# A transformer block on one core: window heads in pairs, and extra tokens' products split behind each half of the gate-up units

## The reference, cut to what matters

```python
h = rms_norm(x, attn_norm);  proj = h @ w_in + b_in
sb = stick_breaking_attention(...)            # 8 heads of 64
sw = sliding_window_attention(...)            # 8 heads of 64, 2 key/value heads, 128 rows a tile, keys of 2 tiles
mixed = concat(rms_norm(sb), rms_norm(sw))
x = x + mixed @ w_out + b_out
x = x + moe(rms_norm(x))                      # 32 experts, 4 a token, 1024 -> 2 x 1024 -> 1024
out = rms_norm(x)

# sliding window, one tile of 128 queries, one head
s = q @ k.T * scale + rel_bias;  p = softmax(concat(s, sink))[..., :-1];  o = p @ v
# expert
gate, up = min(gu[:, :FF], 7), clip(gu[:, FF:], -7, 7)
act = (up + 1) * gate * sigmoid(1.702 * gate);  y = act @ w_down + b_down
```

## Time and profile before

| | us |
|---|---|
| median of 3 runs | 2323.31 |
| runs | 2319.99 to 2324.42 |
| profiled execution, its own time | 2329.55 |
| its span, first to last instruction | 2327.8 |
| TensorE busy | 2142.0 (92%) |
| VectorE busy | 1524.8 (66%) |
| ScalarE busy | 1473.9 (63%) |
| POOL busy | 333.4 (14%) |

### The profile page before, as it was taken

One profiled execution on the slowest core, in us unless ns is written; L12 is line 12 of the kernel. 1 busy time (PEld: TensorE's weight loads), 2 busy tenths in 40 slices (PEclk: granted clock), 3 DMA queues, 4 the chain that ended last, 5 costly groups with the idle time before them and its releaser, 6 DMA issues.

```text
span 2327.8 us, 36220 instructions
## 1 busy us (share of the span) xinstructions
PE 2142.0 (92%) x10647; PEld 1600.9 (69%) x10648; DVE 1524.8 (66%) x1940; ACT 1473.9 (63%) x1976; POOL 333.4 (14%) x327
## 2 busy tenths in 40 slices
PE   5999999998878399999999999999999999999997
PEld 4777777765656277778777677777776677676684
DVE  4455455544444578898879677777776677575685
ACT  4456566643332268888778677777776677575583
POOL 1000000001222211111111111121121111110112
PEclk9999999859888599999999999999999999999996
DMA  6301000111011859999799797897896898696694
GB/s 187 61 19 28 19 10 19 73 46 54 30 56 47 277 191 374 375 377 372 244 378 312 256 369 262 301 373 266 298 371 216 280 333 284 210 367 223 226 358 174
DMA packets 250410, 507.19 MB, mean 218 GB/s; under 512 B 44454, under 2 KB 62676, under 8 KB 250228
## 3 DMA queue, kind: packets, MB, share of 16 engines
q1 hardware_dynamic: 234724, 462.98, 55.2%
q0 software_dynamic: 15632, 43.53, 7.4%
HBM read 470.25 MB, written 38.54 MB: 219 GB/s over the span
## 4 chain that ended last, share of the span: by engine, by line
PE 63%; DVE 9%; DMA 8%; issue 8%; SPq 5%; ACT 4%; POOL 1%; DVEq 0%; ACTq 0%; POOLq 0%
PE bank L963 18%; PE bank L985 11%; PE bank L754 8%; PE bank L803 4%; DMA slot_in<-slot_rows 4%; PE bank L1000 3%; DVE w_low L1740 3%; PE bank L848 3%; PE bank L831 3%; DMA xg<-h_rows,gather_idx 3%; SPq L485 3%; PE bank L1006 3%; PE bank L1021 2%; PE bank L782 2%; SPq L498 1%
## 5 line engine op out<-in xcount | busy, mean ns | idle before, releaser
L1740 DVE TENSOR_TENSOR w_low<-gu_w,w_high 128x1024 fp32r<-128x1024 f32 x528 | 617.3, 1221 | 201.0 <-ACT w_high L1312 197.4
L1312 ACT CAST w_high<-gu_w 128x1024 fp32r<-128x1024 f32 x528 | 531.4, 1049 | 107.5 <-PE bank L985 76.0
L963 PE MATMUL bank<-w_high,x_high 128*128 128x512 f32 x1056 | 415.6, 394 | 2.8 <-DVE w_low L1740 2.8
L963 PE MATMUL bank<-w_high,x_low 128*128 128x512 f32 x1056 | 413.7, 392 | 0.0
L963 PE MATMUL bank<-w_low,x_high 128*128 128x512 f32 x1056 | 413.0, 391 | 0.0
L1740 DVE TENSOR_TENSOR w_low<-dn_w,w_high 128x1024 fp32r<-128x1024 f32 x264 | 315.3, 1226 | 12.1 <-ACT w_high L1312 7.2
L1312 ACT CAST w_high<-dn_w 128x1024 fp32r<-128x1024 f32 x264 | 270.7, 1050 | 18.6 <-PE bank L963 8.6
L985 PE MATMUL bank<-w_high,act_high 128*128 128x512 f32 x528 | 218.9, 415 | 14.5 <-DVE act_low L1754 14.5
L963 PEld LDWEIGHTS bank<-w_high,x_high 128*128 128x128 f32 x1056 | 198.9, 188 | 45.6 <-DVE w_low L1740 3.5
L963 PEld LDWEIGHTS bank<-w_low,x_high 128*128 128x128 f32 x1056 | 198.9, 188 | 42.7
L963 PEld LDWEIGHTS bank<-w_high,x_low 128*128 128x128 f32 x1056 | 198.7, 188 | 42.5
(11 more groups left out here) (227 smaller groups left out, 3282.2 us busy)
## 6 DMA issues: line engine op xcount, KB each, us to landing
gu_w<-in_w_gate_up SPq DMA_DIRECT2D x528, 512.0 KB, 12.3
dn_w<-in_w_down SPq DMA_DIRECT2D x132, 1024.0 KB, 18.4
w_st<-in_w_in SPq DMA_DIRECT2D x14, 512.0 KB, 4.8
xt<-in_x SPq DMA_DIRECT2D x8, 512.0 KB, 4.2
wo_sb<-in_w_out SPq DMA_DIRECT2D x2, 2048.0 KB, 9.9
x<-in_x SPq DMA_DIRECT2D x8, 512.0 KB
residual_rows<-x SPq DMA_DIRECT2D x8, 512.0 KB, 3.6
h_rows<-h SPq DMA_DIRECT2D x8, 512.0 KB
```

Source lines behind the costliest of these rows:

```text
L963: mm = pe.matmul(bank[:, 2 * h + g, :], a[:, k, :], b, start=False, stop=last)
L1312: act.copy(w_high[:, u % RING, :], src).then_inc(high_ready, 1)
L1740: dve.tensor_tensor(w_low[:, u % RING, :], raw, w_high[:, u % RING, :], ALU.subtract).then_inc(split_ready, 1)
```

## The change

The window units become pairs of heads: four steps for a tile in place of eight. `scores` writes two products into one bank, `band` (for `window`) treats both heads, `weights` has two exponents, `turn` transposes four blocks and `values` multiplies them. The work of `out_stage` is bound to steps counted from the start of its tile: `tile_at(step, after)` gives the tile for which `after` steps have passed. The mix transposes come eight steps after the start of their tile, ahead of that step's `turn`; the projection comes in four chunks of four steps (twelve matmuls each). `x2_variance` is split from `normed`, and POOL's order is shifted by one tile.

In the expert stage `over_hidden` is called once for each half: for half 0 behind the first half of units, for half 1 behind the second. With four column tiles each matmul now has 256 columns and there are twice as many; with two tiles the columns stay 512. A new semaphore `over_half` tells that half 0 is through; `refill` waits for it ahead of the first four pairs of `gu_w` loads, and for `over_psum` ahead of the other four. The wait for `y_ready` moves ahead of the first call. `over_rows` reads the gate and up columns with another view of the banks.

```diff
+BAND = NH // 2
+MIX_TURN = 2 * BAND
+LAST = BAND * (NT - 1) + 20
...
-        tD = kb("tD", [P, 2, 2, P], F32, 150)
-        tC = kb("tC", [P, 4, SPAN], F32, 162)
+        tD = kb("tD", [P, 2, 4, P], F32, 150)
+        tC = kb("tC", [P, 2, 2 * SPAN], F32, 162)
...
-        units += [(i, h, "sw") for i in range(NT) for h in range(NH)]
+        units += [(i, j, "sw") for i in range(NT) for j in range(BAND)]
...
+        def tile_at(step, after):
+            t, rest = divmod(step - after, BAND)
+            return t if rest == 0 and 0 <= t < NT else None
...
             def refill(i, e, first):
                 sp.wait_ge(d_gather, 16 * i)
                 load_slots(i, e, first)
-                sp.wait_ge(over_psum, i)
+                sp.wait_ge(over_half, i)
                 sp.sem_inc(sp_passed, 1)
                 for s in range(KT):
+                    if s == 4:
+                        sp.wait_ge(over_psum, i)
+                        sp.sem_inc(sp_passed, 1)
                     sp.wait_ge(split_ready, UNITS * i + (2 * s + 2 - UNITS))
                     load_gu(e, s)
...
-            for t in range(NT + 1):
+            for t in range(NT + 2):
                 if t < NT:
                     for n in range(2 * t, 2 * t + 2):
                         rstd(mix_var, n + 1, mix_rstd, col(40 + n), col(24 + n))
+                if t >= 2:
+                    rstd(x2_var, t - 1, x2_rstd, col(64 + t - 2), col(56 + t - 2))
+                if t < NT:
                     pool.wait_ge(d_x2[t % 2], 16 * (t // 2 + 1))
                     pool.tensor_tensor(x2[:, t % 2], x2[:, t % 2], bout_bc[:], ALU.add).then_inc(xb_ready, 1)
-                if t >= 1:
-                    rstd(x2_var, t, x2_rstd, col(64 + t - 1), col(56 + t - 1))
-                if t >= 2:
-                    write_records(t - 2)
+                if t >= 3:
+                    write_records(t - 3)
...
+                if kind == "sw":
+                    if u == SB:
+                        pe.wait_ge(proj_done, 2 * CHUNKS)
+                    k0, n = max(i - 1, 0) * P, cols // 2
+                    rows = slice(HD * (h // 2), HD * (h // 2) + HD)
+                    for a in range(2):
+                        mm = pe.matmul(out_z[:, n * a:n * a + n], qk_sw[rows, 2 * (h % 2) + a, i * P:i * P + P],
+                                       qk_sw[rows, 4, k0:k0 + n], start=True, stop=True)
...
+            def before_turn(step):
+                t = tile_at(step, MIX_TURN)
+                if t is not None:
+                    turn(("mix", t, 0))
+                    turn(("mix", t, 1))
+                for j in range(1, 4):
+                    t = tile_at(step, 9 + j)
+                    if t is not None:
+                        project(t, range(4 * j, 4 * j + 4))
...
+                else:
+                    before_turn(u - SB)
                 turn(u)
                 if u >= 1:
                     values(u - 1)
                 if u >= SB:
-                    out_stage((u - SB) // NH, (u - SB) % NH)
+                    after_values(u - SB)
...
-            def over_hidden(i, parts):
-                m = P // parts
+            def over_hidden(i, h, parts):
+                m, w = P // parts, HALF // parts
+                bias = bias_f.rearrange("p (g h f) -> p h g f", g=2, h=2)
                 for k in range(-1, KT):
-                    for g in range(parts):
+                    for q in range(parts):
                         lhs = pick_f[:, 0:m] if k < 0 else xo[:, k, 0:m]
...
+                        rhs = bias[:, h] if k < 0 else gu_w[:, h, k]
+                        mm = pe.matmul(over_view(parts)[m * q:m * q + m, h], lhs, rhs[:, :, w * q:w * q + w],
+                                       start=(k < 0), stop=(k == KT - 1))
+                mm.then_inc((over_half, over_psum)[h], 1)
...
                 hidden(i, 0, range(2, KT))
+                pe.wait_ge(y_ready, 2 * i + 2)
+                by_class(n_tok, lambda parts: over_hidden(i, 0, parts))
                 expert_bias(i, 1)
                 hidden(i, 1, range(5))
                 turn_hidden(i, 0)
                 hidden(i, 1, range(5, KT))
-                pe.wait_ge(y_ready, 2 * i + 2)
-                by_class(n_tok, lambda parts: over_hidden(i, parts))
+                by_class(n_tok, lambda parts: over_hidden(i, 1, parts))
```

More of the change, by code:

```diff
@@ L375, in program @@
                 add_groups(("v", m), 4)
+            if tile_at(u - SB, MIX_TURN) is not None:
+                for part in range(2):
+                    add_groups(("mix", tile_at(u - SB, MIX_TURN), part), 4)
             add_groups(u, blocks(u))
-            if u >= SB and (u - SB) % NH == 5 and u - SB >= NH:
+        for step in range(STEPS, LAST):
+            if tile_at(step, MIX_TURN) is not None:
                 for part in range(2):
-                    add_groups(("mix", (u - SB) // NH - 1, part), 4)
-        for part in range(2):
-            add_groups(("mix", NT - 1, part), 4)
+                    add_groups(("mix", tile_at(step, MIX_TURN), part), 4)
         def proj_bank(n):
@@ L915, in _ @@
                 if u >= SB:
-                    out_stage((u - SB) // NH, (u - SB) % NH)
-            values(NU - 1)
-            for t in range(NT, NT + 3):
-                for h in range(NH):
-                    out_stage(t, h)
+                    after_values(u - SB)
+            for step in range(STEPS, LAST):
+                before_turn(step)
+                if step == STEPS:
+                    values(NU - 1)
+                after_values(step)
             for s in range(NT):
@@ L1504, in keep_out, with band @@
                 dve.tensor_copy(o_sb[:, i, P * p:P * p + P], bank[:, 6, 0:P]).then_inc(o_kept, 1)
-            def window(u):
-                i, h, _ = units[u]
-                n = blocks(u) * P
-                tc = tC[:, u % 4, 0:n]
+            def band(u):
+                i, j, _ = units[u]
+                n = blocks(u) * P // 2
                 dve.wait_ge(z_ready, u + 1)
@@ new lines, in out_stage @@
+            def out_stage(step):
+                if step == 0:
+                    keep_out(SB // 2 - 1)
+                if step < 4:
+                    for k in range(2 * step, 2 * step + 2):
+                        dve.wait_ge(wo_high_ready, k + 1)
+                        dve.tensor_tensor(wo_low[:, k], wo_sb[:, k], wo_high[:, k], ALU.subtract).then_inc(wo_split, 1)
+                t = tile_at(step, 20)
+                if t is not None:
+                    places(t)
+                t = tile_at(step, BAND)
+                if t is not None:
+                    sw_sinks(t)
+                t = tile_at(step, 5)
+                if t is not None:
+                    sw_rows(t)
+                t = tile_at(step, 6)
+                if t is not None:
+                    mix_variance(t, 0)
+                    mix_variance(t, 1)
+                t = tile_at(step, 7)
+                if t is not None:
+                    mix_rows(t, 0)
+                    mix_rows(t, 1)
+                t = tile_at(step, MIX_TURN)
+                if t is not None:
+                    mix_low_part(t, 0)
+                    mix_low_part(t, 1)
+                t = tile_at(step, 13)
+                if t is not None:
+                    residual(t)
+                t = tile_at(step, 14)
+                if t is not None:
+                    x2_variance(t)
+                t = tile_at(step, 15)
+                if t is not None:
+                    normed(t)
+                t = tile_at(step, 18)
+                if t is not None:
+                    routing(t)
@@ L1659, in _ @@
             keep_out(SB // 2 - 2)
-            window(SB)
+            band(SB)
             for u in range(SB, NU):
                 if u + 1 < NU:
-                    window(u + 1)
-                out_stage((u - SB) // NH, (u - SB) % NH)
-            for t in range(NT, NT + 3):
-                for h in range(NH):
-                    out_stage(t, h)
-            places(NT - 1)
+                    band(u + 1)
+                out_stage(u - SB)
+            for step in range(STEPS, LAST + 1):
+                out_stage(step)
```

240 lines of the change are left out of this document (111 added, 129 removed).

## The result

The changed kernel takes 2251.36 us (median of 4 runs, 2248.84 to 2252.55), the kernel before 2321.65 us beside it (4 runs, 2318.69 to 2324.42). The medians differ by 70 us, a quotient of 0.9697; the ratio as it was estimated from the runs is 0.9683, with a 95% interval of 0.9663 to 0.9702. Forecast were 2247 us. The profiled execution of after took 2252.55 us, its span is 2250.4.

The account below looks back on a forecast made before the run. TensorE standing still or at its lower clock was taken as the bound. 38.2 us (experts) plus 38 (window stage) gave 76 off 2329.55, 2253.5 profiled, less 6.2 to the median: 2247 us, 8-in-10 range 2228 to 2284.

Parts of the forecast that it names:

- The early load: Expert stage: first eight `gu_w` loads issue about 16 us into an item with extra tokens instead of 31.7.
- the eight late items: Expert stage: plain items behind one with extra tokens lose 45.0 us in all; 43.4 of it forecast as gain.
- The price with up to 32 extra tokens: Expert stage: 144 narrow passes for 72 and entering narrow tiles once more, 0.46 us an item, ten items 4.6.
- T0: First of the window stage's eight row tiles, T0 to T7; held bound by copies of `w_out`, gain 0.
- The clock: Window stage: TensorE's lower clock after stretches without large matmuls, put at 3 us a tile, between 0 and 5.
- `places` (2.3 us from its first line to the `window` behind it): Window stage, first step of a tile: part of VectorE's 6.3 us against TensorE's 5.2, a 1.1 us wait.
- The tail: Between window stage and first expert: 2 us gain, between -5 and 8.
- The window stage kept its time: Rival: waits and lower clock fill what is freed there, only 10 us gained, 2275; chance 0.15.
- the load not forward: Rival, expert stage: the unmoved `dn_w` load holds slots and gather, 45 us stay, 2290; chance 0.08.
- the narrow loads uncovered: Rival, expert stage: each 256-column pass waits for its own weight load, 0.11 us, 2324; chance 0.02.
- the clock for good: Rival: the window stage falls to the lower clock throughout, +115 us, 2362; chance 0.03.
- The better case: Window stage: no lower clock and shorter waits, 15 us more gained, 2232; chance 0.07.

Follow-up runs that it names:

- `small_add`: The changed kernel with POOL's add of the output bias cut to one column of 1024, so the routing differs: 2245.22 us, ratio 0.9658.
- `pool_later`: The changed kernel with POOL's add of x and bias for a tile done one loop later: 2240.18 us, ratio 0.9612.
- `low_first`: The changed kernel with VectorE's `places` moved behind `mix_low_part`: 2240.19 us, ratio 0.9628.
- `late_load`: The changed kernel with SyncE's wait for `over_psum` back ahead of all `gu_w` loads, products still split: 2292.5 us, ratio 0.9864.
- three more edits: The changed kernel with `sw_rows` ahead of `band`, `mix_low_part` ahead of `places` and POOL's add one loop later: 2220.0 us, ratio 0.954.

## Why the prediction was right

**Expert stage, 38.2 forecast, 39.7 measured.** The early load, the idle DMA engines behind it and the eight late items are as argued: 44.75 us (forecast 43.4). My reserve of 0.2 us in each was not needed. The price with up to 32 extra tokens is 0.34 us an item (48.51 to 48.85) where I put 0.46. Of it 0.18 are the passes (2 x 4.02 for 7.86; 8.17 forecast), the other 0.16 lie at the edges of the added block (0.1 to 0.2 estimated, from no row). With up to 64 it is 0.26 (59.95 to 60.21), and I had 0.15. Ten times 0.34 and four times 0.26 make 4.4 (5.2 forecast). Behind an item with extra tokens the gather lands 25.7 us into the next (item 9; 24 to 26 forecast), ahead of TensorE. The Trainium skill ("TensorEngine Tiling (Array Packing)", Instruction Overhead: some 60 cycles for each matmul) would have made the passes cost 18 us in the ten items, as an estimate from that figure. By this trace 72 more passes cost 0.18 us an item, so a fixed cost on each is not seen here. The same page of the Trainium skill (Key Properties) says that a change of tiling mode drains the engine. The trace agrees that both edges of the added block cost something: in item 8 the 48 matmuls ahead of it take 11.02 us, and 10.96 in item 9, which has no such block, the two bias matmuls behind it 0.56 and 0.48, together 0.14 us. No run separates the drain from other causes of it.

**Window stage, 38 forecast, 38.7 measured**, from terms that missed in both directions. The main mechanisms held, but that the sum comes this close is luck: T0 to T2 gave 7.6 us more than forecast, T5 to T7 and the tail 6.4 less.

- T0: forecast 0, fell from 26.39 to 23.02 (3.4). I held it bound by the copies of `w_out`. That reason was wrong: TensorE was busy for 25.36 of these 26.39 us before, and is for 20.70 of 23.02 now. Its idle time grew from 1.0 to 2.3 us, so what fell is the time of the units themselves; why stays open.
- T1 and T2: forecast 20.5 and 30.5, measured 18.08 and 28.74 (6.3 and 4.2 us gained where 3.8 and 2.5 were forecast). T1 is 16.80 us busy where I had doubled the work to 18.4, and waits 1.28 instead of 2.
- T3, T4, T5: 26.5, 30, 31 forecast, 27.13, 29.70, 28.13 measured. Waits of 1.74 (2.0 forecast) and 1.27 (1.1) are as worked out from VectorE's order. (The lines of the earlier trace rows from 653 us on are of T6, which began at 645.27, and not of T5; the wait there is the same in both, 3.74 us.) The clock was the poor term: 3 us a tile forecast; T5 had none (1.00), T3 and T4 0.87 and 0.89.
- T6 and T7: 31 forecast, 33.75 measured for T6. T5 to T7 together, T7 up to the values of its last step, fell from 113.1 to 98.2: 14.9 us (17.4 forecast). The step of the prediction that fails is "`places` (2.3 us from its first line to the `window` behind it)" as a price that doesn't depend on what POOL does. In the step of two heads POOL's add meets the small operations behind `places`, one of them takes 2.1 to 2.3 us, the mix bank wait is 3.2 to 3.4 us instead of 1.1, and the lower clock follows. `small_add` and `pool_later` show that the add does it (T6 29.71 and 29.73 us), `low_first` that `places` ahead of `mix_low_part` passes it on to TensorE. The trace of the kernel before could have told: there the add stretched a norm operation in every tile from T1 on (see the last section).
- The tail: forecast 2 us gain (between -5 and 8), measured 1.9 loss (86.92 to 88.79). It is within what the same kernel does from run to run: T7 and the tail together take 125.1, 124.3 and 130.2 us in its three profiles. What sets this spread stays open.

**Profile to median.** I took the 6.2 us between the profiled execution of before and its median as a property of both kernels. The profiled execution of after lies 1.2 us above its median. 2329.55 - 2252.55 is 77.0 (forecast 76), while the medians differ by 70.3 (2321.65 and 2251.36). 2247 is nothing but 76 off the median of 2323.31 (which came out 1.7 us lower in the four runs beside the change), so the 4 us by which it is too low come from this step: a sum read from one execution that lay 6 us above its median was taken off that median whole. Which stages held those 6 us in that execution isn't shown.

**The rivals.** The window stage kept its time, the load not forward, the narrow loads uncovered and the clock for good are each excluded by a row above (T3 to T5; `late_load` against the change; 4.02 us for 72 passes; clocks of 0.85 to 1.00). The better case was really there, but behind three more edits: 28 to 34 us in the window stage, where I had seen 15.

## What to carry over

Ask of every refill how early the first part of its buffer is free: releasing it in halves bought 45 us here for 4.4 us of narrower passes. When a step of TensorE is made longer, write VectorE's order out again: the operation that TensorE asks for first goes first, and a wait of 1.7 us removed gave 2.4 to 4 where the clock had fallen behind it. And where the one profiled execution lies above the median, a sum read from it may be too large by as much; for steps of a few us compare the stage in the profiles as well as the medians.

## What the runs showed of the hardware

**A POOL operation can hold a VectorE operation until it ends.** Beside POOL's add of 128x1024 (2.36 us) an operation of 128x8 took 2.09 us instead of 0.17, one of 128x28 took 2.30 (at 652.92, ending at 655.22, POOL's at 655.19), one of 128x32 took 2.31. In the kernel before, one of 128x512 took 1.35 at 594.65 beside the add at 593.11, and 0.75 without; it did so in every tile from T1 on (1.33 to 1.72), and in the tail one took 3.36, begun while POOL was still at its norm and held through the add from 733.53 to 735.88 (second fence). The `window` operation, whose first input is a PSUM bank, is not stretched beside the same add (first line, kernel before; the add runs from 593.11 to 595.46):

```profile
594.05 0.48 DVE L1518 CUSTOM_DVE_ANT_0 tC<-bank,swbias,sinks_bc 128x256 f32<-128x256 f32 x1 [2.03 <-PE bank L803]
...
594.65 1.35 DVE L1552 SCALAR_TENSOR_TENSOR o_row<-o_sb,st,mix_bc 128x512 f32<-128x512 f32 x1
```

```profile
733.07 3.36 DVE L1552 SCALAR_TENSOR_TENSOR o_row<-o_sb,st,mix_bc 128x512 f32<-128x512 f32 x1 [3.47 <-POOL st L585]
```

The Trainium skill ("Advanced Engine Details and Errata", GPSIMD Details) says that the Pool engine shares a read and a write interface with VectorE and conflicts with its instructions that have two SBUF inputs or run in a two-port mode. The trace agrees for those with two inputs: the stretched `sw_den`, `eqm` and `o_row` operations read two tensors in SBUF, the free `window` reads a PSUM bank and one tensor in SBUF. The stretched one of 128x28 reads a single tensor; whether it ran in a two-port mode the trace doesn't tell. Not every small operation on SBUF is caught: one of 128x1 beside the same add of before took its usual 0.15 us (L1520 at 594.57). Which forms are, these traces don't settle.

**The clock makes a short wait dear.** T3 with a 1.74 us wait ran at 0.87 and took 27.1 to 27.2 us in six profiles, and at 0.93 and 25.6 in three others; without it, in three, at 1.00 and 23.2. So the wait was worth 2.4 to 4.0 us. Which waits are followed by the lower level isn't fixed: T5 of the changed kernel has waits of 1.27 and 1.74 us and keeps 1.00.
